# A hybrid attention and DeltaNet block: VectorE's rotation of queries and copies of keys and values moved to other quarters of each mixer turn

## The reference

```
proj = h @ w_in + b_in                      # aq, ak, av | dq, dk, dv, dz | db, da | ga, gb
aq = rope(aq); ak = rope(ak)                # 32 heads of 64, 4 key/value heads
o_att = sliding_window_sink_attention(aq, ak, av, sinks)   # window 128 = 2 chunks of 64
qkv = silu(causal_depthwise_conv([dq, dk, dv]))            # 4 taps
q, k = l2_normalize(q) * 128**-0.5, l2_normalize(k)        # 16 heads of 128
# gated delta rule, two chunks of 128 here (64 in the reference; the same function):
#   a = (k*beta) k^T * decay * strict;  (I + a)^-1;  u, w;  a scan over the chunks with state S
#   o_i = (q * exp(gcum)) S + (q k^T * decay) v_new
o_dn = gated_rms_norm(gated_delta_rule(q, k, v, g, beta), dz)
merged = sigmoid(ga) * (o_att @ w_br_att) + sigmoid(gb) * (o_dn @ w_br_dn)
h = layer_norm(2**0.25 * h + merged @ w_out)
h = layer_norm(2**0.25 * h + swiglu(h) + sigmoid(h @ w_ple_gate + b) * (p @ w_ple_proj))
```

## Time and profile before

| what | value |
|---|---|
| runs of the kernel | 1992.9 us median of 3 (1990.43, 1992.9, 1994.19) |
| profiled execution, its own time | 1992.74 us |
| its span in the profile | 1990.6 us |
| TensorE matmuls busy | 1948.9 us, 98% |
| TensorE weight loads busy | 1697.5 us, 85% |
| VectorE busy | 1287.9 us, 65% |
| ScalarE busy | 980.5 us, 49% |
| POOL busy | 28.3 us, 1% |
| mean granted clock of TensorE | 0.996 |
| DMA | 176 GB/s on average |

### The profile page before, as it was taken

The page is one execution under the profiler, slowest core; times in us unless marked ns, Lnnn a source line. Parts: engine busy times, 40 slices in busy tenths (PEclk is TensorE's granted clock), DMA queues, the critical chain, the costliest instruction groups (busy, mean ns, idle before and its releaser), DMA issues.

```text
span 1990.6 us, 30302 instructions
## 1 busy us (share of the span) xinstructions
PE 1948.9 (98%) x10869; PEld 1697.5 (85%) x10869; DVE 1287.9 (65%) x2355; ACT 980.5 (49%) x1874; POOL 28.3 (1%) x52
## 2 busy tenths in 40 slices
PE   8999999999999999999999999999999999999996
PEld 7889999999999988888888878888888888888885
DVE  6558788788778766565566697555555555555555
ACT  4446445445544535455544464544454444444442
POOL 1000000000000000000000000000000000000000
PEclk9999999999999999999999999999999999999998
DMA  8666345355345455666557546556555555665551
GB/s 310 201 178 156 116 123 128 109 132 132 105 111 135 134 171 182 239 190 201 192 188 254 190 157 205 190 189 190 189 189 189 190 190 190 214 208 191 194 196 74
DMA packets 203605, 349.53 MB, mean 176 GB/s; under 512 B 6705, under 2 KB 72449, under 8 KB 202513
## 3 DMA queue, kind: packets, MB, share of 16 engines
q1 hardware_dynamic: 200272, 334.13, 51.2%
q0 software_dynamic: 3264, 14.47, 4.3%
HBM read 344.19 MB, written 2.10 MB: 174 GB/s over the span
## 4 chain that ended last, share of the span: by engine, by line
PE 87%; DVE 9%; issue 2%; ACT 1%; DVEq 0%; DMA 0%; SPq 0%; ACTq 0%
PE dense L547 23%; PE dense L549 23%; PE dense L548 23%; PE dense L535 4%; PE dense L536 4%; PE dense L537 4%; DVE lo L1304 2%; PE chain L696 2%; PE chain L675 1%; PE chain L766 1%; DVE cv L1479 1%; DVE Um L1581 1%; PE chain L951 0%; ACT sE L1143 0%; PE chain L776 0%
## 5 line engine op out<-in xcount | busy, mean ns | idle before, releaser
L1304 DVE TENSOR_TENSOR lo<-raw,hi 128x512 fp32r<-128x512 f32 x1256 | 849.6, 689 | 513.5 <-ACT hi L994 512.1
L994 ACT ACTIVATE hi<-raw 128x512 fp32r<-128x512 f32 x1256 | 780.7, 631 | 704.8 <-PE dense L549 622.1
L547 PE MATMUL dense<-hi,xh 128*128 128x512 f32 x1376 | 540.1, 393 | 1.7 <-DVE xl L1819 1.1
L549 PE MATMUL dense<-lo,xh 128*128 128x512 f32 x1376 | 536.2, 390 | 0.0
L548 PE MATMUL dense<-hi,xl 128*128 128x512 f32 x1376 | 535.7, 389 | 0.0
L547 PEld LDWEIGHTS dense<-hi,xh 128*128 128x128 f32 x1376 | 258.6, 188 | 55.2 <-DVE xl L1819 2.0
L549 PEld LDWEIGHTS dense<-lo,xh 128*128 128x128 f32 x1376 | 258.4, 188 | 54.5
L535 PE MATMUL dense<-xh,hi 128*128 128x256 f32 x1024 | 304.4, 297 | 0.0
L548 PEld LDWEIGHTS dense<-hi,xl 128*128 128x128 f32 x1376 | 258.7, 188 | 52.4
L537 PE MATMUL dense<-xh,lo 128*128 128x256 f32 x1024 | 289.8, 283 | 0.0
L536 PE MATMUL dense<-xl,hi 128*128 128x256 f32 x1024 | 289.6, 283 | 0.0
(11 more groups left out here) (289 smaller groups left out, 1518.0 us busy)
## 6 DMA issues: line engine op xcount, KB each, us to landing
raw<-in_w_in_dram SPq DMA_DIRECT2D x116, 1024.0 KB, 5.0
raw<-in_w_ffn_gate_dram SPq DMA_DIRECT2D x44, 1024.0 KB, 5.1
raw<-in_w_ffn_up_dram SPq DMA_DIRECT2D x44, 1024.0 KB, 5.1
raw<-in_w_ffn_down_dram SPq DMA_DIRECT2D x44, 1024.0 KB, 5.0
raw<-in_w_br_att_dram SPq DMA_DIRECT2D x16, 1024.0 KB, 5.0
raw<-in_w_br_dn_dram SPq DMA_DIRECT2D x16, 1024.0 KB, 5.0
raw<-in_w_out_dram SPq DMA_DIRECT2D x16, 1024.0 KB, 5.0
raw<-in_w_ple_gate_dram SPq DMA_DIRECT2D x16, 1024.0 KB, 4.9
```

The lines of the kernel that those rows point to most:

```text
L547: pe.matmul(o, ah, hi[:, s, :], start=(k == 0), stop=False)
L549: mm = pe.matmul(o, ah, lo[:, s, :], start=False, stop=(k == nk - 1))
L994: act.activation(hi[:, pos.slot(n), :], raw[:, slot, off:off + 512], ACT.Copy).then_inc(sem("hi_ready"), 1)
L1304: dve.tensor_tensor(lo[:, pos.slot(n), :], raw[:, slot, off:off + 512], hi[:, pos.slot(n), :].bitcast(F32), ALU.subtract).then_inc(sem("lo ...
```

## The change

It concerns three pieces of VectorE's work in a turn, and two waits that keep tiles safe.

- The rotation of queries (was attention stage -2, quarter 1) becomes `rotate(i, j)`. Turn i calls it at quarter 20 for the queries of the next turn, j = (i + 1) % 8. It waits for `pt1`, since it uses `sE` and `sO` as scratch.
- The copies of keys and values (was attention stage 5, quarter 8) become `keys_values(i, j)`, called at quarter 21 for the next turn. It waits for `pv`.
- Both are called once ahead of turn 0. In turn 7 they work on pair 0 again, and the result is not used: there are nine of each in place of eight.
- `qd` is scaled at chain stage 6, quarter 8, behind the mask of the first level's `Yz`, and no longer at the end of stage 3, quarter 5.
- POOL's first two loads of gate biases and VectorE's first `gate_sum` also wait for the ninth rotation (and POOL for the ninth copy).

```diff
                 if n < 2:
                     pool.wait_ge(sem("att_out"), PAIRS)
+                    pool.wait_ge(sem("qrot"), PAIRS + 1)
+                    pool.wait_ge(sem("kvS"), PAIRS + 1)
...
                     dve.scalar_tensor_tensor(bv[:], C[:, 3, :].rearrange("p (x c) -> p x c", x=4), 0.5,
                                              each(row[:, 5, :], 4), ALU.mult, ALU.mult).then_inc(sem("bv"), 1)
-                    dve.wait_ge(sem("egb"), p + 1)
-                    dve.tensor_tensor(qd[:], cq[:, :, P:T], qd[:], ALU.mult).then_inc(sem("qdec"), 1)
                 elif k in (6, 8, 10, 12, 14, 16):
...
+                    if n == 1:
+                        dve.wait_ge(sem("egb"), p + 1)
+                        dve.tensor_tensor(qd[:], cq[:, :, P:T], qd[:], ALU.mult).then_inc(sem("qdec"), 1)
...
             def att_k(k, i):
-                if k == -2:
-                    t = i % TT
-                    q = qbuf[:, ds(i, 1), :].rearrange("p o (h c) -> p (o h) c", c=32)
...
-                elif k == 5:
-                    for b in range(2):
...
-                elif k == 7:
+                if k == 7:
...
+            def rotate(i, j):
+
+
+                if i >= 0 if isinstance(i, int) else True:
+                    dve.wait_ge(sem("pt1"), i + 1)
+                t = j % TT
+                q = qbuf[:, ds(j, 1), :].rearrange("p o (h c) -> p (o h) c", c=32)
+                tc = flat(sE[:]).rearrange("p (h c) -> p h c", c=32)
+                ts = flat(sO[:]).rearrange("p (h c) -> p h c", c=32)
...
+                dve.tensor_tensor(tc, q, cos, ALU.mult).then_inc(sem("q_cs"), 1)
+                dve.tensor_tensor(ts, q, sin, ALU.mult).then_inc(sem("q_cs"), 1)
+                dve.wait_ge(sem("q_cs"), 2 * i + 4)
...
+                dve.tensor_tensor(qr[:, :, 0:32], tc[:, :, 0], ts[:, :, 1], ALU.subtract)
+                dve.tensor_tensor(qr[:, :, 32:64], tc[:, :, 1], ts[:, :, 0], ALU.add).then_inc(sem("qrot"), 1)
+
+            def keys_values(i, j):
+
+                if i >= 0 if isinstance(i, int) else True:
+                    dve.wait_ge(sem("pv"), i + 1)
+                for b in range(2):
+                    R = slice(64 * b, 64 * b + 64)
+                    dve.tensor_scalar(kS[R, b, :], kTall[R, ds(j, 1), :].rearrange("p o n -> p (o n)"), 1.0, None,
+                                      ALU.mult)
+                dve.tensor_scalar(vS[:], vall[:, ds(j, 1), :, :].rearrange("p o n d -> p (o n) d"), 1.0, None,
+                                  ALU.mult).then_inc(sem("kvS"), 1)
...
                     att_k(k - ATT_LAG, i)
+                    if k == 20:
+                        rotate(i, (i + 1) % PAIRS)
+                    elif k == 21:
+                        keys_values(i, (i + 1) % PAIRS)
                     qk_front(k, i)
...
             dve.wait_ge(sem("kS_zero"), 1)
+            rotate(-1, 0)
+            keys_values(-1, 0)
             mixer_turn(0, False)
...
                 if n == 0:
                     dve.wait_ge(sem("att_out"), PAIRS)
+                    dve.wait_ge(sem("qrot"), PAIRS + 1)
```

More of the change, by code:

```diff
@@ L1659, in att_k @@
                                       ALU.mult).then_inc(sem(f"prob{n}"), 1)
+            def rotate(i, j):
[5 more added lines that the diff above has]
+                ts = flat(sO[:]).rearrange("p (h c) -> p h c", c=32)
+                cos = cst[:, ds(C_COS + 32 * t, 32)].unsqueeze(1).to_broadcast([P, 16, 32])
+                sin = cst[:, ds(C_SIN + 32 * t, 32)].unsqueeze(1).to_broadcast([P, 16, 32])
+                dve.tensor_tensor(tc, q, cos, ALU.mult).then_inc(sem("q_cs"), 1)
+                dve.tensor_tensor(ts, q, sin, ALU.mult).then_inc(sem("q_cs"), 1)
+                dve.wait_ge(sem("q_cs"), 2 * i + 4)
+                tc = tc.rearrange("p (h a) c -> p h a c", a=2)
+                ts = ts.rearrange("p (h a) c -> p h a c", a=2)
+                dve.tensor_tensor(qr[:, :, 0:32], tc[:, :, 0], ts[:, :, 1], ALU.subtract)
[9 more added lines that the diff above has]
+                                  ALU.mult).then_inc(sem("kvS"), 1)
             def mixer_turn(i, chain):
```

## The result

| | before | changed |
|---|---|---|
| runs, median | 1992.41 us of 5 (1990.43 to 1994.19) | 1979.15 us of 5 |
| ratio | | 0.9932, 95% interval 0.9917 to 0.9948 |
| profiled execution, its own time | 1992.74 us | 1978.29 us |
| span | 1990.6 us | 1976.5 us |
| TensorE matmuls busy | 1948.9 us | 1944.9 us |

One of the five executions of the changed kernel took 9085 us; it is left out of the ratio, and the other four lie between 1978.14 and 1980.17, with a median of 1978.7. The change makes the kernel 0.7% faster. VectorE runs seven more instructions, those of the ninth rotation and copies, and is busy for 2 us more. TensorE runs the same 10869 matmuls; its idle time falls from 41.7 to 31.6 us, and the other 4.0 us of the 14.1 by which the span is shorter lie in its busy time, in which the dip of the clock and the modelled ends of matmuls count.

The account below looks back on a forecast made before the run. The prediction took TensorE's wait for `Yz`, late in VectorE's queue, as the bound: 1992.74 - 12.2 (wait) - 1.6 (clock dip) + 0 (added work) = 1978.9 us, given as 1979.1 us, range 1976.5 to 1984.0.

Parts of the forecast that it names:

- What bounds the loop: First-level `inv_x` matmuls on TensorE wait 1.48 us for `Yz`, held only by VectorE's backlog of earlier work.
- Seven times 1.74 us: Turns 1 to 7: stretch with `inv_x` takes 6.45 us stalled, 4.71 unstalled; removing the wait gains 12.2 us in all.
- The margin of 0.8 us at `Yz`: First level: `Yz` would end at 272.68, TensorE wants it at about 273.5, so the wait goes entirely.
- The walk through quarters 20 to 22: Beside the scan: moved rotation and copies, 2.68 us, fit into VectorE's idle time; `S` and `bv` stay in time, cost 0.
- The 0.1 to 0.2 us for register instructions: Rotation at quarter 20: if margins are gone, this much cost a turn, at most 1.4 us in all.
- The side that would have made it slower: Quarters 20 to 22: the 2.68 us delay `S` and `bv` in full, costing 16.7 us, total 1997.4 us; chance 0.03.
- The dip, 1.6 us: One turn of 72.97 us, clock 0.50 behind the long wait: expected gone, gaining 1.6 us, bounds 0 and 3.2.
- What I called luck: Clock in the loop: a dip needs the long wait and luck, since six other turns have that wait without one.
- The total: Whole kernel: 12.2 and 1.6 us off, cost 0, giving 1979.1 us; wait and dip both gone had chance 0.52.
- What was costed at nothing: Rotation and copies ahead of turn 0, their ninth run in turn 7, POOL's later gate-bias loads, moved `qd`: cost 0.
- Taking them out only gives VectorE room: Copies of keys and values, 0.67 us behind `Yz` and before the split: they cost the wait nothing.

Follow-up runs that it names:

- the kernel with 2.66 us more: The changed kernel with the two products of the rotation made three times at quarter 20: 1997.06 us, ratio 1.0021 to the kernel before.
- the kernel with the maxima moved: The changed kernel with attention's row maxima moved to quarters 12 and 13, where VectorE waits for TensorE: 1970.35 us, ratio 0.9891 to the kernel before.

## Why the prediction was right

- **What bounds the loop** ("bound by VectorE's queue and by nothing else"). Right: taking 2.01 us out of the queue ahead of `Yz` removed the wait, 0.33 us shortened it by 0.3, and 0.67 us behind `Yz` did nothing.
- **Seven times 1.74 us.** Right, 71.37 - 69.63. The idle time in the waits' list would have given 10.4 us; comparing a stalled stretch with the same work unstalled gave the right size. The Trainium skill, "Perfetto Trace Analysis", section "Identifying the Most-Contended Engine", says that busy time of pipelined matmuls is no good measure of how close TensorE is to its roofline. The traces agree: in a turn the idle time fell by 2.33 - 0.86 = 1.47 us, and the turn by 1.74.
- **The margin of 0.8 us at `Yz`.** Right, 0.75 us.
- **The walk through quarters 20 to 22.** Right to 0.02 us: from the start of the rotation, `S` was forecast 309.28 - 306.27 = 3.01 us later and came 3.00 later; `bv` 5.02 and 5.00. The 0.1 to 0.2 us for register instructions, which I had taken from no row, did not show in any run. The side that would have made it slower was true of larger work only: the first loss comes with 0.27 us more a turn, and the kernel with 2.66 us more is slower than the one before.
- **The dip, 1.6 us.** Right that it goes with the long wait: no profile of a kernel whose waits are 0.7 us or less has one. What I called luck stays unexplained, since a wait of 1.2 us had dips in one kernel and none in another. In the median the term is an average over executions. The changed kernel plus seven turns of 1.74 us is 1991.3 us, and the medians of before in four sets of runs are 1992.4 to 1992.9, so dips make up 1.1 to 1.5 us of them (an estimate from these numbers). By another measure it is more: five of 51 executions of before have a mean granted clock of 0.997, the others 0.996 or 0.995 (the profiled one with one dip 0.996, the one with two 0.995), and these five took 1990.3 to 1990.9 us, which is 1.5 to 2.6 us under those medians. The size of this term is therefore known to about 1 us only. Of the two sections of the Trainium skill's page "TensorE: Matmul & The Clock Gate" that I weighed, "A second HAM failure mode: psum-queue depth-cycling" says that short idle spells between matmul groups can let the clock fall back. The traces agree in this, with dips behind waits of 1.2 to 1.8 us, though the page's case is another, a kernel that cycles through PSUM banks. "Why this matters for your kernels" warns only of gaps longer than these, so it does not cover the dips of this kernel.
- **The total.** That 1979.1 met 1979.15 so closely is luck. Four executions of the changed kernel spread over 2.0 us. The forecast took 13.8 us off 1992.9, the median of the first three runs; the medians of all runs differ by 1992.41 - 1979.15 = 13.3.
- **What was costed at nothing.** Turn 0: VectorE's pair ahead of it started at 133.69, and TensorE waited for no split. POOL's gate biases were issued at 654.85, 0.32 us ahead of the loop's last correction of `bv`, and before at 661.89, 7.73 us ahead of it; so they come 7.4 us later in the turn, where some 7 were expected, and TensorE waited for nothing there. The end of the span did grow by 0.4 us with the ninth rotation and copies (above), which I had not seen coming, and which the execution's own time hardly shows.
- **What I said only of the whole change and not of its parts.** "Taking them out only gives VectorE room" is true of the copies where they stand alone behind `Yz`, as in the run of the copies alone. With `qd` in front of them and the rotation still at quarter 1 they held the scores up by 0.15 us.

The expectation that failed was that of `qd` alone (71.0 us a turn for a measured 71.24), for this reason. The total of `qd` with the copies came out at 1988.62 for 1990.4 because I had kept the dips of before in it, and its profile has none.

## What to carry to other kernels

Where one engine runs in a fixed order and another waits for it, list the queue ahead of the late instruction: its data may have been there for microseconds, and then any work that stands ahead of it and is needed later can go to where the engine waits for others. What is taken out beyond the length of the wait brings nothing, so one move of 2.0 us did what three did. Walk the new place forward instruction by instruction, since the room there ends sharply (0.27 us here). Size such a wait by the same work stalled and unstalled, not by the idle time in a list: here 1.48 us of idle time cost 1.74.

## What the runs showed that I had not expected

- A dip of the clock to 0.50 costs a turn of this kernel 1.2 to 1.6 us (73.24 - 72.03; 72.97 - 71.37). It comes behind waits of TensorE of 1.2 to 1.8 us: in six of the 28 turns, of four profiles, whose waits are 1.48 us or more, and in two of 14 whose wait is 1.16 or 1.18 us. In 35 turns whose waits are 0.7 us or less, or that have none, there is no dip. The spread of a kernel's runs does not follow from this: it is 3.8 us before and 1.05 us for `qd` and copies together, but 1.0 us with the products made three times, which has a dip in its profile, and 2.45 us in the kernel with the maxima moved, which has neither wait nor dip in its own.
- The effect of a part depends on what else is moved: `qd` alone 0.13 us a turn, the copies alone nothing, the two together 0.33, and beside the rotation both nothing.
